# Masks of picked scores on ScalarE, pooled means three units later, and tiles that start 64 bytes further on

## What is computed

```
h = h + 1/2 SwiGLU_1(RMSNorm(h))
u = RMSNorm(h);  u @ W_in -> q | latent c | index q, k, weights | z | memory q | 3 gates
A: score[t,s] = sum over 8 heads of iw[t,h] * relu(iq[t,h] . ik[s]);  causal;
   the 128 highest of each row are attended to (others masked), softmax with a bias, 8 heads
B: z in 4 groups of 64 channels: trailing mean over 2, 4, 8, 16 tokens, minus z, then a 64x64 matrix
C: 4-head cross-attention into 256 memory tokens
h = h + W_out( sum of sigmoid(gate_i) * (branch_i @ W_branch_i) )
h = h + 1/2 SwiGLU_2(RMSNorm(h))
```

## Time and profile before

| | |
|---|---|
| median of 3 runs | 2253.84 us (2250.84 to 2254.43) |
| profiled execution | 2246.63 us, of which the span of its instructions is 2244.8 us |
| PE busy | 2216.6 us, 99% of the span |
| DVE, ACT, POOL busy | 953.5, 523.6, 1325.7 us |
| slots of the combined projection and of the branches, layer 0 | about 388 to 686 us from the span's start; layer 1 the same some 1107 us later |

### The profile page before, as it was taken

The page is one execution under the profiler, slowest core; times in us unless marked ns, Lnnn a source line. Parts: engine busy times, 40 slices in busy tenths (PEclk is TensorE's granted clock), DMA queues, the critical chain, the costliest instruction groups (busy, mean ns, idle before and its releaser), DMA issues.

```text
span 2244.8 us, 31758 instructions
## 1 busy us (share of the span) xinstructions
PE 2216.6 (99%) x10262; PEld 1805.1 (80%) x10262; DVE 953.5 (42%) x1716; ACT 523.6 (23%) x1013; POOL 1325.7 (59%) x884
## 2 busy tenths in 40 slices
PE   9999999999999999999999999999999999999996
PEld 6888888877788888888888888888778888888885
DVE  5331344578855433023333223536877453321334
ACT  3110112443553210001111101125445432100111
POOL 7666657644436665665766566584444376656653
PEclk9999999999999999999999999999999999999998
DMA  5243223222113222332333332232211132223222
GB/s 183 96 134 107 94 80 118 93 69 68 62 54 107 94 94 86 101 103 76 105 102 121 110 107 94 76 130 78 69 62 66 48 121 95 93 83 105 99 79 76
DMA packets 68219, 209.88 MB, mean 93 GB/s; under 512 B 7536, under 2 KB 10776, under 8 KB 67864
## 3 DMA queue, kind: packets, MB, share of 16 engines
q1 hardware_dynamic: 64128, 203.62, 27.7%
q10 hardware_dynamic: 3992, 5.00, 0.7%
HBM read 206.48 MB, written 3.68 MB: 94 GB/s over the span
## 4 chain that ended last, share of the span: by engine, by line
PE 93%; DVE 4%; issue 1%; ACT 1%; DMA 1%; POOL 0%; DVEq 0%; ACTq 0%; POOLq 0%; SPq 0%
PE bank L608 29%; PE bank L607 28%; PE bank L606 28%; PE obank L859 1%; PE sbank L804 1%; PE tbank L826 1%; DVE picks L1356 1%; DVE top L1354 1%; PE obank L617 0%; PE sbank L796 0%; PE sbank L779 0%; DMA h<-in_xT 0%; PE obank L843 0%; PE sbank L757 0%; PE sbank L810 0%
## 5 line engine op out<-in xcount | busy, mean ns | idle before, releaser
L541 POOL TENSOR_TENSOR wL<-raw,wH 128x1024 fp32r<-128x1024 f32 (+3 forms) x424 | 896.0, 2113 | 35.4
L538 POOL TENSOR_SCALAR wH<-raw 128x1024 fp32r<-128x1024 f32 (+3 forms) x424 | 397.4, 937 | 842.1 <-PE bank L608 820.1
L608 PE MATMUL bank<-u0L,wH 128*128 128x512 f32 x1376 | 542.1, 394 | 0.0
L607 PE MATMUL bank<-u0H,wL 128*128 128x512 f32 x1376 | 539.3, 392 | 0.0
L606 PE MATMUL bank<-u0H,wH 128*128 128x512 f32 x1376 | 536.1, 390 | 0.0
L607 PEld LDWEIGHTS bank<-u0H,wL 128*128 128x128 f32 x1376 | 258.3, 188 | 61.1 <-issue 1.0
L606 PEld LDWEIGHTS bank<-u0H,wH 128*128 128x128 f32 x1376 | 258.3, 188 | 58.4 <-issue 1.0
L608 PEld LDWEIGHTS bank<-u0L,wH 128*128 128x128 f32 x1376 | 258.7, 188 | 51.5
L606 PE MATMUL bank<-u1H,wH 128*128 128x512 f32 x704 | 293.2, 416 | 0.0
L608 PE MATMUL bank<-hidL,wH 128*128 128x512 f32 x704 | 277.4, 394 | 0.0
L607 PE MATMUL bank<-hidH,wL 128*128 128x512 f32 x704 | 276.0, 392 | 0.0
(11 more groups left out here) (189 smaller groups left out, 2177.8 us busy)
## 6 DMA issues: line engine op xcount, KB each, us to landing
raw<-in_wA SPq DMA_DIRECT2D x176, 512.0 KB, 3.2
raw<-in_wM SPq DMA_DIRECT2D x96, 512.0 KB, 3.3
raw<-in_wB SPq DMA_DIRECT2D x64, 384.0 KB, 3.0
raw<-in_wB SPq DMA_DIRECT2D x64, 320.0 KB, 2.9
raw<-in_wR SPq DMA_DIRECT2D x32, 256.0 KB, 2.5
mem<-in_memT SPq DMA_DIRECT2D x2, 1024.0 KB, 6.9
near_bias<-bias_rows ACTq DMA_DIRECT2D x2, 1024.0 KB, 6.4
outT<-gate_a SPq DMA_DIRECT2D x4, 512.0 KB, 2.7
```

The lines of the kernel that those rows point to most:

```text
L538: pool.tensor_scalar(wH[:, w, 0:cols], raw[:, slot, 0:cols], 1.0, 0.0, ALU.mult, ALU.add).then_inc(rounded, 1)
L541: pool.tensor_tensor(wL[:, w, 0:cols], raw[:, slot, 0:cols], wH[:, w, 0:cols].bitcast(F32), ALU.subtract).then_inc(split_done, 1)
L607: pe.matmul(dst, b, hi[:, k, :], start=False, stop=False)
L608: mm = pe.matmul(dst, a, lo[:, k, :], start=False, stop=last and i == len(tiles) - 1)
```

## The change

Three things change. The mask: DVE only tells by the semaphore `picked` that a block's last round is done; ACT, after the step in which that happens (`MASK_AFTER`: steps 13, 24 and 41), runs one relu over `picks` in place, with a scale and a bias that give 0 where picked and 2^100 elsewhere. DVE waits for `mask_ready` before the block's first A step and subtracts the mask instead of adding it. The means: their five pieces stand at the ends of slots 14 to 18 instead of 11 to 15. The tiles: `eps` gets a second column for the relu's bias and 192 bytes instead of 128, so that every tile behind it starts 64 bytes further on. Then `sg`, `u0`, `hid`, `y` and all tiles of the stages start at multiples of 128 bytes; `rms`, `ssq`, `ta`, `over_d`, `over_r` and `eps` stay as they were.

```diff
-PICKED = -3e38
+PICKED = -2.0 ** 127
+MASKED = 2.0 ** 100
...
-MEANS_AT = {("in", 11 + piece): piece for piece in range(5)}
+MEANS_AT = {("in", 14 + piece): piece for piece in range(5)}
...
-    c[:, K_CAUSAL:K_CAUSAL + P] = np.where(np.arange(P)[None, :] <= np.arange(P)[:, None], 0.0, NEG)
+    c[:, K_CAUSAL:K_CAUSAL + P] = np.where(np.arange(P)[None, :] <= np.arange(P)[:, None], 0.0, -NEG)
...
-        eps = sb("eps", [P, LINE // 4])
+        eps = sb("eps", [P, LINE // 4 + LINE // 8])
...
+                    if i in MASK_AFTER:
+                        mask = picks[MASK_AFTER[i]][:, :]
+                        act.wait_ge(picked, l * (QB - 1) + MASK_AFTER[i])
+                        act.activation(mask, mask, ACT.Relu, scale=MASKED / -PICKED, bias=eps[:, 1:2]
+                                       ).then_inc(mask_ready, 1)
...
-            dve.memset(eps[:, :], EPS).then_inc(weights_set, 1)
+            dve.memset(eps[:, 0:1], EPS).then_inc(weights_set, 1)
+            dve.memset(eps[:, 1:2], MASKED).then_inc(weights_set, 1)
...
                     if n == TOPK // 8 - 1:
-
-                        own.done(dve.tensor_scalar(picks[qb][:, :], picks[qb][:, :], PICKED, NEG,
-                                                   ALU.not_equal, ALU.mult))
-                        own.wait()
+                        dve.sem_inc(picked, 1)
...
+                            if a:
+                                dve.wait_ge(mask_ready, l * (QB - 1) + a)
```

More of the change, by code:

```diff
@@ L186, with last_rounds @@
 S_INDEX = {u: n for n, u in enumerate(S_USES)}
+def last_rounds():
+    done, at = 0, {}
+    for slot in SLOTS:
+        for _, kind, n, picks in PLAN[slot]:
+            if kind == "step":
+                for qb in range(1, QB):
+                    if done < qb * (TOPK // 8) <= done + picks:
+                        at[n] = qb
+                done += picks
+    assert sorted(at.values()) == list(range(1, QB))
+    return at
+MASK_AFTER = last_rounds()
 def both(i, at):
@@ L395, in trunk @@
         score_added = sem("score_added")
+        picked = sem("picked")
+        mask_ready = sem("mask_ready")
         pooled = sem("pooled")
@@ L663, in hidden @@
                             if first and i == 1:
-                                pe.wait_ge(weights_set, 3)
+                                pe.wait_ge(weights_set, 4)
                                 pe.wait_ge(ssq_added, l * 24 + ssq_count)
@@ L951, in root @@
                 act.preload_act_table_set("natural_log_exp_and_others")
-                act.wait_ge(weights_set, 3)
+                act.wait_ge(weights_set, 4)
                 act.wait_ge(norm_mean, n)
@@ L1377, in add_score @@
                         dve.scalar_tensor_tensor(picks[qb][:, qb * P:width], src[:, qb * P:width], w, causal,
-                                                 ALU.mult, ALU.add).then_inc(score_added, 1)
+                                                 ALU.mult, ALU.subtract).then_inc(score_added, 1)
                         own.wait()
@@ L1437, in logits @@
                                                               far_bias[:, head(b):head(b) + 1], mask[:, 0:near],
-                                                              ALU.add, ALU.add))
+                                                              ALU.add, ALU.subtract))
                         own.wait()
-                        dve.tensor_tensor(p[:, near:width], src[:, near:width], mask[:, near:width], ALU.add
+                        dve.tensor_tensor(p[:, near:width], src[:, near:width], mask[:, near:width], ALU.subtract
                                           ).then_inc(logits_read, 1)
```

## The result

| | before | after |
|---|---|---|
| median | 2252.34 us (2246.24 to 2254.43, 6 runs) | 2272.70 us (2271.83 to 2273.70, 6 runs) |
| profiled execution | 2246.63 us | 2273.70 us |
| PE busy | 2216.6 us | 2242.4 us |

The ratio is 1.009, with a 95% interval from 1.0078 to 1.0102. The changed kernel is slower by 20 us, where 2239.2 us was forecast, 14.6 us faster than before. The result lies outside the range, on the side that had a chance of 0.08.

What follows compares the result with a forecast made beforehand. PE, busy 99% of the span, was taken as the bound, through matmul pace and few waits. Tiles -14.4 and stage -0.2 made -14.6 us; against the median of 2253.8 the forecast was 2239.2 us, range 2235 to 2246.

Steps and rivals of the forecast that it cites:

- Term 1: SwiGLU's 2080 triples reading `u0` and `hid`, plus some others, gain u1's pace from the new tile start: -14.4 us.
- Rival (c): SwiGLU's 2080 triples: shifted tiles hold PE at the unsettled pace, 0.013 us more each, up to 2281 us; chance 0.03.
- The check that the prediction proposed: Sign of being right: in SwiGLU the three mean durations of L606 to L608 are 389 in the new profile.
- The rival that rested on the pages: SwiGLU: a tile's start costs nothing, pace stays 686.6 ns, only the stage is left, 2253.6 us; chance 0.19.
- Term 2: Slot 13: PE's 1.53 us wait for `add_score` ends as the means leave the scores, -1.6 us a layer.
- Term 3: Slots 14 to 18: the arriving means add 5.2 us on DVE; PE stands 2.0 us later at B, slot 13's gain included.
- Term 4: Block 2's mask, L1360: ACT's relu replaces DVE's 2.50 us, taking back 2.1 of 2.4 us of PE waits a layer.
- The stage in sum: Net of masks and means in the slots: +2.0 - 2.1 = -0.1 us a layer, -0.2 in all.
- Rival (b): Slots 14 to 18: the pieces cost 8.0 us instead of 5.2, B starts at 529.1, 2244.8 us; chance 0.10.

## Why the prediction was wrong, step by step

**Term 1, the tiles: wrong in sign.** -14.4 us was forecast; +23.7 follows from the paces in the profiled executions, and the medians of the tiles alone give +20. What failed is the step "what differs is the tile that streams: `u0` starts 64 bytes past a multiple of 128, `u1` on one". The two tiles differed in two things at once, their own start and their distance to the weights: 64 and 0. The change puts `u0` on the same kind of start and at distance 128, a third case, which no row of before contained. Two things that the prediction had in hand pointed the other way and were argued down. The 256-column triples were without a cost, which contradicts a cost of the start. Rival (c) named the right pair of operands, "if streaming rows and weights that both start on 128 bytes met each other". It got 0.03 because `u1` ran through 58 triples in peace, and its condition was indeed not the cause: `u1` and the weights both start on 128 bytes and have the fastest pace. `u1` and `u0` after the change differ in the distance to the weights, which (c) did not have. That its price of 13 ns a triple, taken from `u1` behind an interruption, lies near the 10.6 measured is luck.

The 256-column matmuls go the other way. In the kernel with the tiles moved by 192, the memory's projection, PE's timeline:

```profile
376.76 0.28 PE L709 MATMUL bank<-yH,wH 128*128 128x256 f32 x1
...
377.12 0.28 PE L709 MATMUL bank<-yH,wH 128*128 128x256 f32 x1
```

0.36 us a triple, where the earlier trace rows have 0.34. The distance that is best for 512 columns is the worse one here.

The check that the prediction proposed, a mean duration of 389, would also have misled. The page of the kernel moved by 192 has

```profile
L606 PE MATMUL bank<-u0H,wH 128*128 128x512 f32 x1376 | 537.4, 391 | 0.0
```

which is 1 ns above, while its starts are 2.2 ns closer to each other. Modelled ends can't rank two paces that lie this near.

The Trainium skill, "TensorE: Matmul & The Clock Gate" (Step-by-step: what each phase is for), says that weight loads and streamed rows come through two independent read ports, and "SBUF — State Buffer" (Who interferes with whom) that PE never waits on anyone. By these pages no distance could matter. Here the measurement decides: 680 to 700 ns, by where one tile lies relative to the other. The rival that rested on the pages, no change from the tiles, failed as the forecast did. The 216 ns that the prediction took from the Trainium skill, "TensorE: Matmul & The Clock Gate" (Back-to-back issue gap), are in that section the gap of an isolated matmul; for a stream with weight loads it has about 131 ns at 512 columns. No run here shows that: the least is 680 ns for three, 227 each.

**Term 2, the means leave the scores: right.** -1.6 a layer; 1.8 was regained at slot 13 in the changed kernel, 1.65 in the one with the means alone at distance 0, and no wait for `add_score` was left.

**Term 3, the means arrive: right in kind, too small.** The net at B was forecast as +2.0 and measured as +3.25 in layer 0 of the kernel without the tile change. The timeline of DVE after the change shows the pieces, some of their small instructions left out:

```profile
498.91 2.05 DVE L1415 TENSOR_TENSOR za<-z 128x1022 f32<-128x1022 f32 x1
...
501.73 0.30 DVE L1459 TENSOR_TENSOR sbank<-sbank,near_bias 128x128 f32<-128x128 f32 x1 [0.70 <-PE sbank L825]
...
507.49 1.20 DVE L1415 TENSOR_TENSOR gate_bc<-za 128x1020 f32<-128x1020 f32 x1
...
514.68 0.69 DVE L1415 TENSOR_TENSOR za<-gate_bc 128x508 f32<-128x508 f32 x1 [0.15 <-DVE picks L1383]
...
515.48 0.68 DVE L1415 TENSOR_TENSOR gate_bc<-za 64x504 f32<-64x504 f32 x1
...
522.84 0.67 DVE L1433 SCALAR_TENSOR_TENSOR za<-za,z 64x496 f32<-64x496 f32 x1
523.43 0.16 DVE L1435 TENSOR_TENSOR za<-za,cst 64x16 f32<-64x16 f32 x1
523.62 0.59 DVE L1437 TENSOR_TENSOR za<-za,z 64x16 f32<-64x16 f32 x1
524.25 0.67 DVE L1433 SCALAR_TENSOR_TENSOR gate_bc<-gate_bc,z 64x496 f32<-64x496 f32 x1
524.84 1.23 DVE L1435 TENSOR_TENSOR gate_bc<-gate_bc,cst 64x16 f32<-64x16 f32 x1
526.11 0.17 DVE L1437 TENSOR_TENSOR gate_bc<-gate_bc,z 64x16 f32<-64x16 f32 x1
...
526.64 0.29 DVE L1466 TENSOR_TENSOR probs<-sbank,cst 128x128 f32<-128x128 f32 x1
```

The sum had 5.2 us more on DVE, less 0.3 for the mask of block 1: 4.9. In layer 0 of the kernel without the tile change DVE takes up the unit of slot 14 at 489.89 instead of 491.83 and is through for B at 527.31 instead of 522.97: 6.3 us more between the two. Pieces 0 to 2 take 2.1, 1.3 and 1.6 us with their copies, 5.0 together, where 4.7 had been allowed (3.8 of their own and 0.9 of waiting). Piece 3 shows the largest single loss: its instructions of 16 columns, 0.16 and 0.17 us when alone, took 0.59 and 1.23, 1.5 us of waiting together, while POOL's split of the next half unit ran from 523.58 to 524.20 and from 524.28 to 526.04. But the same piece had waited for POOL in its old place too, and that wait was in the 522.97 from which the sum started. DVE before:

```profile
494.50 1.52 DVE L1409 SCALAR_TENSOR_TENSOR za<-za,z 64x496 f32<-64x496 f32 x1
...
503.00 0.65 DVE L1409 SCALAR_TENSOR_TENSOR za<-za,z 64x496 f32<-64x496 f32 x1
```

1.52 - 0.65 = 0.87 us of waiting before, so that piece 3 adds 0.6, near the 0.5 allowed. What the sum lacked altogether is what DVE does around the pieces: it idles 0.7 us for PE behind piece 0, at 501.73, where piece 3 with its 2.8 us had stood and no wait was, and it has restarts of 0.15 to 0.19 us at pieces 1 and 2, some 0.3 more in all than the restarts that are gone. 0.3 + 0.1 + 0.7 + 0.3 = 1.4 us make up the difference of 6.3 and 4.9.

The place was also named second where it comes first. PE's main wait is not at B but at the Q step of slot 18, which needs DVE to have read the logits (L1466, at 526.64) that stand behind piece 3: 3.24 us in each layer, while B waits 1.7 us in one layer and not at all in the other.

**The clock, which the sum did not have.** After the wait, in layer 0 of the changed kernel, PE's timeline and its windows:

```profile
526.99 2.08 PE L817 MATMUL sbank<-q,pr 64*128 64x128 f32 x16 [3.24 <-DVE probs L1466]
529.00 0.79 PE L627 MATMUL bank<-u1H,wH 128*128 128x512 f32 x1
529.59 0.63 PE L628 MATMUL bank<-u1H,wL 128*128 128x512 f32 x1
530.02 0.63 PE L629 MATMUL bank<-u1L,wH 128*128 128x512 f32 x1
```

```profile
523.00:527.00 4.00, 0.76 (x7) 0.94 0.04 16
527.00:531.00 4.00, 4.00 (x21) 0.50 0.39 131
531.00:535.00 4.00, 4.00 (x16) 0.70 0.00 0
535.00:539.00 4.00, 4.00 (x20) 1.00 0.02 4
```

PE had been idle but for 0.76 us of four when the granted clock fell to 0.50, the lower of its two levels, 1.2 GHz. The matmuls of the next units start 0.43 us apart instead of 0.23. That swallows the wait at B, and the layer ends 2.40 us late where layer 1, which kept its clock and waited 1.7 us at B, ends 1.21 late. This drop, of 6.8 us, therefore costs about 1.2 us, not the full price of the slow matmuls, since DVE held B up anyway. A shorter one costs next to nothing: without the tile change the clock is low for 3.4 us in layer 1 (above), and the layer ends 1.08 us late against 1.04 for layer 0, which kept its clock. At distance 0, the kernels with the whole change and with the means alone have a drop in both layers, 3.4 us in layer 0 and 6.8 in layer 1; with the whole change the layers end 1.23 and 2.28 us late.

**Term 4, the mask of block 2: right.** -2.1 a layer forecast, -2.2 measured with the masks alone. ACT's relu, all six of them:

```profile
L1155 ACT ACTIVATE picks<-picks,eps x6: 510/602/723, 514.6 to 1751.7; 128x256 f32<-128x256 f32 x2, 128x384 f32<-128x384 f32 x2, 128x512 f32<-128x512 f32 x2
```

0.51 to 0.72 us, where the earlier trace rows gave 0.62 for 384 columns, and the view of DVE's waits has no row for `mask_ready`.

**The stage in sum**: -0.1 us a layer was forecast; +1.0 to +1.1 was measured without the tile change, +1.5 (3.0 for both layers) at distance 0, with the clock low in both layers. Of the 35 us between the forecast's -14.6 and the measured +20.4 the stage is 2 to 4; the rest is term 1. Rival (b), the pieces at full price, gave B at 529.1 where about 527.5 came: neither it nor the forecast had the size.

## What to carry to other kernels

When two tiles differ in pace, list everything in which they differ, their distance to the operand they are paired with too, before one of the differences is made a term for 2080 triples; a pad that moves all tiles and one that moves the partner alone cost one run each and tell them apart. On a kernel bound by PE, try the streamed tiles at each distance of 0, 64, 128 and 192 bytes (mod 256) to the weights for the width that matters: 2232 to 2275 us here for one line of padding. Work that leaves one wait of PE should be followed to the next place where PE needs that engine, and a wait of some 3 us counts with the half-speed matmuls that may stand behind it.

## What the runs showed of the hardware that was not expected

- The pace of 512-column float32 matmuls depends on the distance of the streamed tile to the weights' tile, modulo 256 bytes: 680, 686.7, 697 and 700 ns for three, at a granted clock of 1.00. Why was not found, nor whether `wH`, `wL` or both matter, since they lie at the same distance.
- At distance 64 there are two paces, 686.7 and 700 ns, each held for a whole stretch of some 270 triples. The kernel moved by 256 has one slow stretch and took 2251.09; the profiled executions of before and of the 64 bytes ahead of all tiles have none and took 2246.63 and 2245.65; the one of masks and means without the tiles has one, and the kernel with the weights moved has two. All four lie in the first half of a layer's first SwiGLU. Steps of 3.6 us fit the scatter of the kernel before (in one set of eight runs: five at 2246 to 2247, two at 2250 to 2251, one at 2253), while the kernel at distance 0 scatters by 0.3 us over four runs. For the runs without a profile this is inferred, not shown.
- A DVE instruction of 16 columns with two inputs in SBUF took 1.23 us beside POOL's split, against 0.17 alone: a small instruction paid 1.06 us, where piece 0 over 1022 columns had paid 1.4.
- Behind 3.2 us of waiting PE's granted clock fell to half in six layers out of eight, for 3.4 or for 6.8 us; behind the 1.5 us at slot 13 of the kernel before it stayed at 1.00.
